# Moving the gate-matrix turns of a fused block four weight slabs earlier, with Pool's share, the lists and the sparse dots

## The reference, cut to what matters

```python
def peer_ffn(h, peer_wq, peer_keys, peer_u, peer_v):
    q = (ht @ peer_wq).reshape(T, PEER_HEADS, 2, PEER_DH)
    s = jnp.einsum('thpd,hpkd->thpk', q, peer_keys)
    sv, si = lax.top_k(s, PEER_TOPK)
    cand = sv[..., 0, :, None] + sv[..., 1, None, :]        # 16 x 16 candidates
    top, pos = lax.top_k(cand, PEER_TOPK)
    eidx = jnp.take_along_axis(cidx, pos, axis=-1)
    g = jax.nn.softmax(top, axis=-1)
    # for each token and each of its 8 x 16 picks
    a = jax.nn.gelu(jnp.einsum('td,thkd->thk', hb, peer_u[ib]))
    return jnp.einsum('thk,thkd->td', gb * a, peer_v[ib])
```

## Time and profile before

| | before |
|---|---|
| median of 3 runs | 1592.05 us (1588.79 to 1592.96) |
| the profiled execution | 1593.64 us, its span 1591.8 us |
| TensorE busy | 1553.2 us, 98% |
| VectorE busy | 1355.9 us, 85% |
| ScalarE busy | 631.5 us, 40% |
| Pool busy | 593.5 us, 37% |
| granted TensorE clock, mean | 0.996 |

### The profile page before, as it was taken

How to read it: one execution, slowest core, us unless ns; L and a number is a source line. 1 busy time by engine, 2 the same in 40 slices (tenths; PEclk the granted TensorE clock), 3 DMA queues, 4 the chain that set the end, 5 groups by cost and what they waited for, 6 DMA issues and landing times.

```text
span 1591.8 us, 23427 instructions
## 1 busy us (share of the span) xinstructions
PE 1553.2 (98%) x8490; PEld 1348.1 (85%) x8490; DVE 1355.9 (85%) x2600; ACT 631.5 (40%) x972; POOL 593.5 (37%) x421
## 2 busy tenths in 40 slices
PE   8999999999999999989999999999999999999998
PEld 4777678887889999988999888888888888888887
DVE  6899787765699889998985798899888998998886
ACT  4433835235334344434443333333333333333332
POOL 0000100102435624465403355565455555555540
PEclk9999999999999999999999999999999999999999
DMA  8421255654424669998889999999999999999992
GB/s 333 154 100 41 77 193 171 236 188 146 151 88 124 194 231 311 353 305 252 252 283 365 403 371 376 378 380 397 377 370 381 379 388 390 377 382 373 376 376 95
DMA packets 195277, 442.38 MB, mean 278 GB/s; under 512 B 57761, under 2 KB 100961, under 8 KB 195042
## 3 DMA queue, kind: packets, MB, share of 16 engines
q1 hardware_dynamic: 130480, 248.97, 43.7%
q0 software_dynamic: 52880, 175.73, 30.1%
q10 hardware_dynamic: 11810, 16.27, 2.9%
HBM read 395.75 MB, written 45.11 MB: 277 GB/s over the span
## 4 chain that ended last, share of the span: by engine, by line
PE 74%; DVE 14%; DMA 6%; issue 2%; ACT 2%; SPq 1%; DVEq 0%; ACTq 0%
PE bank L1767 13%; PE bank L1768 12%; PE bank L1769 12%; PE bank L2118 10%; PE bank L2119 10%; PE bank L2120 10%; DVE sb_w_lo L1125 3%; DMA sb_stage<-v_dram 3%; DVE sb_spare L1636 2%; DVE sb_x L1586 2%; PE bank L2097 1%; PE bank L2023 1%; DMA sb_stage<-u_dram 1%; DVE sb_x L1582 1%; ACT sb_w_hi L772 1%
## 5 line engine op out<-in xcount | busy, mean ns | idle before, releaser
L772 ACT ACTIVATE sb_w_hi<-sb_stage 128x1024 fp32r<-128x1024 f32 x324 | 343.0, 1060 | 463.3 <-PE bank L2120 242.7
L1767 PE MATMUL bank<-sb_act_hi,sb_w_hi 128*128 128x352 f32 (+1 forms) x1408 | 488.4, 347 | 2.9 <-DVE sb_w_lo L1125 2.2
L1768 PE MATMUL bank<-sb_act_lo,sb_w_hi 128*128 128x352 f32 (+1 forms) x1408 | 482.3, 343 | 0.0
L1769 PE MATMUL bank<-sb_act_hi,sb_w_lo 128*128 128x352 f32 (+1 forms) x1408 | 481.9, 342 | 0.0
L1125 DVE TENSOR_TENSOR sb_w_lo<-sb_stage,sb_w_hi 128x1024 fp32r<-128x1024 f32 x290 | 354.3, 1223 | 103.4 <-ACT sb_w_hi L772 100.8
L2118 PE MATMUL bank<-sb_w_hi,sb_mix_hi 128*128 128x512 f32 x768 | 300.4, 391 | 6.4 <-DVE sb_mix_lo L1625 6.4
L2119 PE MATMUL bank<-sb_w_lo,sb_mix_hi 128*128 128x512 f32 x768 | 299.9, 390 | 0.0
L2120 PE MATMUL bank<-sb_w_hi,sb_mix_lo 128*128 128x512 f32 x768 | 299.3, 390 | 0.0
L1767 PEld LDWEIGHTS bank<-sb_act_hi,sb_w_hi 128*128 128x128 f32 x1408 | 265.4, 189 | 22.8 <-issue 4.4
L1768 PEld LDWEIGHTS bank<-sb_act_lo,sb_w_hi 128*128 128x128 f32 x1408 | 265.6, 189 | 16.5 <-issue 0.5
L1769 PEld LDWEIGHTS bank<-sb_act_hi,sb_w_lo 128*128 128x128 f32 x1408 | 265.4, 188 | 15.1
(11 more groups left out here) (265 smaller groups left out, 1971.0 us busy)
## 6 DMA issues: line engine op xcount, KB each, us to landing
sb_stage<-u_dram SPq DMA_DIRECT2D x128, 512.0 KB
sb_stage<-v_dram SPq DMA_DIRECT2D x128, 512.0 KB
sb_stage<-w_front_dram SPq DMA_DIRECT2D x68, 512.0 KB
sb_scr<-w_ada_dram POOLq DMA_DIRECT2D x32, 512.0 KB, 4.4
a_scratch<-sb_scr ACTq DMA_DIRECT2D x80, 192.0 KB
sb_scr<-a_scratch SPq DMA_DIRECT2D x16, 960.0 KB
g_old_scratch<-sb_scr SPq DMA_DIRECT2D x11, 1280.0 KB
sb_scr<-g_old_scratch SPq DMA_DIRECT2D x16, 880.0 KB
```

What stands on the lines that cost most here:

```text
L772: nc.scalar.activation(w_hi[:, slot, :], stage[:, slot, :], ACT.Copy).then_inc(w_round, 1)
L1767: nc.tensor.matmul(out, w_hi[:, slot, w], rhs_hi[:, dc, :], start=(i == 0), stop=False)
L1768: nc.tensor.matmul(out, w_hi[:, slot, w], rhs_lo[:, dc, :], start=False, stop=False)
L1769: last = nc.tensor.matmul(out, w_lo[:, slot, w], rhs_hi[:, dc, :], start=False, stop=(i == len(dcs) - 1))
```

## The change

All positions behind the top-k move four slabs earlier. Pool forms low halves up to slab 16 instead of 20, the exponentials are taken at slab 15 instead of 20, the lists are turned behind slab 18 instead of 22, and the turns occupy slabs 20 to 67 instead of 24 to 71. The two halves of the sparse dots are spread over 16 and 20 units, from unit 2 and unit 22 of the turns, instead of 12 and 12, from 2 and 14. The early dots stay at the last eight slabs before slab 80. Pool's fifth gather of the laps waits for the first gate product (`c_mul`).

```diff
-S_FIRST = (2, 14)
-S_UNITS = 12
+S_FIRST = (2, 22)
+S_UNITS = (16, 20)
...
-EXP_SLAB = 20
-POOL_SLABS = 20
-LIST_SLAB = 22
+EXP_SLAB = 15
+POOL_SLABS = 16
+LIST_SLAB = 18
...
-G_FIRST = 24
+G_FIRST = 20
...
-    return [S_HALF * half + d for d in range(S_HALF) if 0 <= k == d * S_UNITS // S_HALF]
+    return [S_HALF * half + d for d in range(S_HALF) if 0 <= k == d * S_UNITS[half] // S_HALF]
...
                             elif n == 1:
                                 pool.wait_ge(row_used, EARLY_DOTS)
+                            elif n == 4:
+                                pool.wait_ge(c_mul, 1)
                             gather(n % ROWS, which, pick)
...
-                        if it * G_UNITS + b == S_FIRST[half] + S_UNITS:
+                        if it * G_UNITS + b == S_FIRST[half] + S_UNITS[half]:
                             act.wait_ge(s_used, S_HALF * (half + 1))
...
-                        if it * G_UNITS + b == S_FIRST[half] + S_UNITS + 1:
+                        if it * G_UNITS + b == S_FIRST[half] + S_UNITS[half] + 1:
                             sparse_weights(half)
...
             for b in range(EARLY - G_LAST):
                 split_unit(FRONT + G_LAST + b + 2, (FRONT + G_LAST + b + 2) % RING)
-                if b < EARLY_DOTS:
-                    early_dot(b)
+                if b >= EARLY - G_LAST - EARLY_DOTS:
+                    early_dot(b - (EARLY - G_LAST - EARLY_DOTS))
```

2 lines of the change are left out of this document (1 added, 1 removed).

## The result

| | before | after |
|---|---|---|
| median | 1591.17 us (17 runs) | 1594.83 us (17 runs, 1589.58 to 1597.38) |
| ratio of after to before | | 1.0020, 95% interval [1.0014, 1.0027] |
| the profiled execution | 1593.64 us, span 1591.8 | 1591.63 us, span 1589.5 |

The change costs 3.2 us by the ratio and 3.7 by the medians, where 0.6 us of gain was forecast. So spans can't be compared here; the stages can. One execution of a later experiment (the kernel before with its dots at (2, 18)) took 8773 us; its ratio is taken without it.

A forecast was written before the change was run, and what follows sets the result against it. TensorE was taken as busy nearly throughout, with VectorE bounding the first two turns. +0.4 us at the second unit of the laps, then -1, gave -0.6 on the median: 1591.5 us, own range 1587 to 1597.

The forecast's parts named there:

- Step 1: Slabs 16 to 19, ahead of the turns: TensorE waits, +5.5 us (3 to 8), and +0.8 for four slower slabs.
- Step 2: The turns: spreading the sparse dots cuts TensorE's waits for VectorE, -9.1 us, from -4 to -13.
- Step 3: Second-half sparse adds end later, early gathers follow late and slab 75 waits: +7.6 us, from 0 to 16.
- Step 4: Handover to the laps: TensorE reaches the first v slab at 877; the second unit starts at 881.8 against 881.38.
- The laps: Behind the handover: 1 us gained, from 0 to 3, of some 3.5 us lost near 915 and 988.
- The slower one: Late sparse adds: if they take 57 us, the row comes 8 us later, giving 1599.5 us; chance 0.22.
- The faster rival: Sparse adds through in under 44 us: slab 75 waits for nothing, giving 1585 us; chance 0.20.
- three signs of being wrong: No TensorE gap between slabs 74 and 76; slab 72 over 4 us off 833.4; first v slab waits 3 us.

## Why the prediction was wrong

**Step 1, ahead of the turns: right.** Predicted 5.5 us and 0.8 for the four slow slabs; measured 4.6 and 5.6 (the pairs of profiles). The waits stand where they were put: 1.32 us before slab 18 (predicted 1.4) and 2.27 before the lists (predicted 2.6). The 1.84 us from which the clock's share was taken is some 0.3 too much, since the first v slab takes 4.12 us at a full clock and not 3.84.

**Step 2, the turns: right.** Predicted -9.1, measured -9.5 to -10.2. Waits of 0.7 to 1.4 us at seven batches were said, 6.4 us in all; the profile has five of 0.53 to 1.54, and the turns lose 5.4. No wait of over 1.54 us is left, as said, though TensorE was busy for 37.4 to 38.5 of 40 us per window and not for over 38. The runs with unmoved turns add that all of it comes from the dots. What the prediction did not ask is which of its two edits wins it: with the turns where they were the same gain costs nothing ahead of them.

**Step 3, the late adds: right in mechanism and time.** Weights at 790.5 (near 795 was said), adds of 47.9 us (49.4), the first gather at 839.1 (844.4), its row after 4.3 us (4.4), slab 75 waiting 4.82 us (6.0). That the 4.4, taken from plain loads, fits the row so well is in part luck: with the dots at (2, 20) in the kernel before the same row took 10.0 us. By the Trainium skill (DMA: Bandwidth & Descriptors, Anatomy of one DMA — SWDGE (gpsimd) path) the estimate for the row was 3.2 us; the trace shows 4.3. The last nine adds took 1.55 us each where the earlier trace rows have 1.66 to 2.13. The Trainium skill (SBUF — State Buffer, SBUF: two separate sides) says that certain VectorE instructions lock GpSimd out of the port over which it writes descriptors. The rows fit that in the main: the five adds of after that overlap a one-hot product took 2.09 to 2.51 us, and those beside nothing 1.55; but one with only a low half beside it took 2.28, so which instructions do it stays open. It was worth little, since three adds wait 4.5 to 5.5 us for the group before.

**Step 4, the handover: this step failed.** The prediction took 877 for TensorE's arrival, 3.84 us for the first v slab and 1 us for late tiles, and argued that "the transfers had 6 us of waiting TensorE to catch up in". They did not catch up. A load needs a free stage slot, a slot comes free with a low half of VectorE, and VectorE was held by the same late row; Pool's gathers were held too. So while TensorE waited, the DMA engines idled as well (share 0.66 from 828 to 848 us, 0.90 over 62 us), and the stretch was one in which they had no time to spare. The wait of 3.25 us stayed as 2.68, followed by a slow v slab: 5.8 us from its start to the next unit, 2.0 over the 3.84. Together 4.7 us, against 1 (0.3 of it is the first v slab that takes 4.12 us without any wait). Less what slab 75 and its clock came cheaper than the 7.6, the handover lost 11.4 to 11.6 against 8.6 in the prediction. That is 2.9 us of the miss of 4.3. The sentence that the wait on the first product "keeps four gathers of 0.5 MB out of the way of the first tiles" was wrong: in the trace of after this wait holds no gather, and without it the same sum was lost.

**The laps: wrong, by 1.7 us.** The prediction took 1 us as gained behind the handover, because before lost 3.5 us near 915 and 988. The laps gained nothing (+0.7): in before the waits near 915 are 0.49 and 1.48 us, in after 0.99 and 1.44. That they belong to the same debt fits the kernel before with dots at (2, 20): there the first v slab waits 6.12 us and no wait of over 0.3 us follows up to 1060 us.

**The rivals.** The slower one was priced for adds that take longer. They didn't, and the kernel came out slower all the same: the true rival was one that isn't in the list, that what is lost ahead of slab 75 is not shared with the handover but added to it. It would have shown in the windows of before: the DMA engines were full from 848 us on, so there was nothing to catch up with. The earlier trace rows end at 836 us, just ahead of that.

```profile
848.00:872.00 24.00, 24.00 (x146) 24.00 (x145) 12.39 (x17) 7.65 (x11) 8.09 (x7) 1.00 1.04 394
```

The faster rival had the adds through in time and the kernel at 1585. Its condition was met by experiment, and slab 75 then waited for nothing: 1587.94 us with the dots at (2, 20), 1582.94 without the second half's adds.

**Its own signs.** Of the three signs of being wrong, the first did not come: TensorE has its gap at slab 75. The second came: slab 72 starts near 828.8 us (811.91 + 0.9 + 4 x 4.00), 4.6 off 833.4, but 2.6 of that is the front of this profile, the same program, which was that much faster than in the rows. The third nearly came: the first v slab waits 2.68 us.

**Open.** Why the debt shows up as a wait at 910 us and not earlier once the first v slab doesn't wait was not followed further. Which part of the 11 us the gathers' lateness causes, and which the idle stage slots, wasn't separated either; both have the one cause.

## What to carry to other kernels

When an edit puts a wait into a stretch, look at the DMA share of the stretch behind it before counting on a catch-up. If the share is already 1.0 there, an engine's wait that also stops loads and gathers is paid again later, and reordering only moves the place where it is paid. And take a two-part edit apart: here the spreading of the dots gained 6 to 10 us in the turns by itself, and up to 6 us of the whole time where the adds stayed in time; at the place that was chosen, (2, 22), it lost 7 in the kernel before. The move of the turns, which came with it, was 3.7 us slower by itself.

## What the runs showed of the hardware

TensorE's pitch changes at a full granted clock. Up to the wait of slab 75 the slabs of after run at 4.00 us, and behind it the same slabs run at 3.80 us, at a granted clock of 1.00 in both stretches. Between them, after the idle 4.82 us, stand two windows with a granted clock of 0.86 and 0.85, that is, in part at the lower of the two levels, 1.2 GHz, in part at 2.4. These windows of after and ScalarE's evacuations behind them:

```profile
836.00:848.00 12.00, 7.18 (x38) 6.88 (x37) 4.17 (x6) 2.82 (x4) 7.41 (x7) 0.86 0.66 192
848.00:860.00 12.00, 12.00 (x67) 12.00 (x67) 9.87 (x13) 2.83 (x4) 7.64 (x5) 0.85 1.02 376
```

```profile
860.17 0.47 ACT L996 ACTIVATE sb_scr<-bank 128x352 f32<-128x352 f32 x1 [2.39 <-PE bank L1771]
863.97 0.47 ACT L996 ACTIVATE sb_scr<-bank 128x352 f32<-128x352 f32 x1 [2.39 <-PE bank L1771]
867.77 0.47 ACT L996 ACTIVATE sb_scr<-bank 128x352 f32<-128x352 f32 x1 [2.38 <-PE bank L1771]
```

They stand 3.80 us apart, those of the earlier trace rows at the same work 4.00. In the kernel with the product's rounding first, the matmuls of 352 columns start 0.167 us apart ahead of the wait of 4.99 us, then 0.293 apart for 5.4 us (some 2.4 us lost), then 0.16:

```profile
852.09 0.48 PE L1773 MATMUL bank<-sb_act_hi,sb_w_lo 128*128 128x352 f32 x1
852.38 0.35 PE L1771 MATMUL bank<-sb_act_hi,sb_w_hi 128*128 128x352 f32 x1
852.57 0.33 PE L1772 MATMUL bank<-sb_act_lo,sb_w_hi 128*128 128x352 f32 x1
852.74 0.33 PE L1773 MATMUL bank<-sb_act_hi,sb_w_lo 128*128 128x352 f32 x1
```

Neither the slower clock nor the wait is needed for the change. In the run without the wait on the first product the pitch went from 0.167 to 0.16 behind a wait of 1.97 us with the clock at 1.00 (844 to 856 us). With the moved turns and dots at (2, 20) it did so with no wait at all, over the 18 matmuls of the first v slab, which take 4.12 us here:

```profile
866.68 0.33 PE L1770 MATMUL bank<-sb_act_lo,sb_w_hi 128*128 128x352 f32 x1
866.85 0.33 PE L1771 MATMUL bank<-sb_act_hi,sb_w_lo 128*128 128x352 f32 x1
867.01 0.39 PE L2120 MATMUL bank<-sb_w_hi,sb_mix_hi 128*128 128x512 f32 x1
...
871.13 0.33 PE L1769 MATMUL bank<-sb_act_hi,sb_w_hi 128*128 128x352 f32 x1
871.30 0.32 PE L1770 MATMUL bank<-sb_act_lo,sb_w_hi 128*128 128x352 f32 x1
871.46 0.32 PE L1771 MATMUL bank<-sb_act_hi,sb_w_lo 128*128 128x352 f32 x1
```

What makes the pitch of 0.167 from the first gate matmul on, and what ends it, no run here tells.
